# Sixteen of 22 chunks of three feed-forward down-projections as two-by-two blocks with seven block products

## The chip, the cores and the metric

The kernel runs on one core of a Trainium2 chip. Its time is the device time of one execution in microseconds (us). Engines are called by their full names here; in rows, PE is TensorE's products and PEld its weight loads, DVE is VectorE, ACT ScalarE, POOL GpSimd and SP SyncE, which issues most of the DMAs.

## What is computed

Four layers over 256 tokens of width 1024. Each layer has a token mixer (forgetting attention, a state-space layer, mean pooling, forgetting attention again) and then a SwiGLU feed-forward of width 2816; behind each comes a LayerNorm of the scaled residual:

```python
def swiglu(x, w1, w3, w2):
    return (jax.nn.silu(x @ w1) * (x @ w3)) @ w2
    ...
        h = layer_norm(DN_ALPHA * h + m, ln_g[i, 0], ln_b[i, 0])
        h = layer_norm(DN_ALPHA * h + swiglu(h, ffn_w1[i], ffn_w3[i], ffn_w2[i]), ln_g[i, 1], ln_b[i, 1])
```

All is float32.

## The kernel before

Weights come as 370 tiles of 128x1024, 512 KB each, in the order of their use. SyncE loads them into four places `raw`. A float32 value is multiplied as two halves of type float32r: ScalarE rounds a tile to its high half (`hi`, L615), VectorE subtracts that from the tile for the low half (`lo`, L998), and TensorE makes three products, high by high, high by low and low by high. Activations are split in the same way. The halves of a tile lie in `whi` and `wlo` (four places) or in `ext` (four more); which, and whose use frees it, is worked out once by `ring()`. SyncE reloads a `raw` place when the low half of its tile is made; so in layers 1 to 3 the split runs `AHEAD` = 4 tiles further ahead of TensorE than in layer 0.

Each engine's program is written out by hand, and engines wait for each other on counting semaphores: `w_hi` and `w_lo` count tiles rounded and subtracted, `w_used` those TensorE is done with. `hi_to`, `lo_to` and `split_to` split tiles in order up to a number.

**Feed-forward** (`ffn` on each engine). The 2816 hidden channels are 22 chunks of 128. A chunk has two up tiles, `up1` into bank 4 and `up3` into bank 5 (`fm`, L1603 to L1605: 24 products of 256 columns each), and one down tile (`tm`, L1612 to L1618: 12 of 512 columns, for two token blocks and two halves of the width, added up in banks 0 to 3 over all chunks). Chunks 0 and 1 are made token by token (`four_tiles`, L1721) as the LayerNorm delivers, and their `h` is turned (`h_turned`, L1775). Then come `up1(2)`, `up3(2)`, `down(0)`, `down(1)`, and from chunk 3 on up, up and the chunk before's down. ScalarE makes `silu` of bank 4 (L695), VectorE multiplies it by bank 5 into `hval` (`gate`, L1146), ScalarE rounds that to `hhi`, VectorE subtracts for `hlo` (L1150). `up1(c)` waits for chunk c-1's silu, since it writes the same bank, and `up3(c)` for chunk c-1's gate. The last three down tiles stand bank by bank in `tm_end` (L1655), so that VectorE can add bank after bank to the scaled residual in `x_tm` (`residual`, L1014) and begin the LayerNorm.

**GpSimd** works out the state-space tables (`s5_parameters`, `s5_turns`) in layer 0 and issues a few DMAs; in layers 1 to 3 it computes nothing but one copy. In layer 0, VectorE also makes these tables: nine scalings (`s5_scale`) from the attention on, and 48 pieces (`s5_tables`), three a chunk, in the feed-forward. In the attention (`fox`) ScalarE and VectorE copy the values from banks 0 to 3 to `vt` in step 0 of the pairs of heads, behind other copies.

## Time and profile before

| | us |
|---|---|
| runs, median (lowest to highest of 3) | 1180.45 (1180.45 to 1181.71) |
| the profiled execution's own time | 1180.47 |
| its span, first to last instruction | 1178.7 |
| TensorE busy in it | 1157.2 |
| VectorE busy | 819.7 |
| ScalarE busy | 599.1 |
| GpSimd busy | 158.2 |

The span is divided into 40 slices of 29.5 us in the page's second part. Products on TensorE overlap, so the time from one product's start to the next one's start says what it costs, not its own duration. The mean granted clock of TensorE is 0.998 of full speed.

### The profile page before, as it was taken

The numbers are of one execution on the slowest core, as the hardware profiler recorded it, in microseconds if no ns is written. First come the engines' busy times: TensorE is split into PE (matmuls) and PEld (weight loads), VectorE is DVE, ScalarE is ACT, GpSimd is POOL, SyncE is SP. The second block draws the span as 40 slices with busy tenths as digits, with TensorE's granted clock in tenths as the row PEclk, the third lists the DMA queues.
The fourth block names the chain that finished last, engine by engine and source line by source line (L and its number), as shares of the span: only waits on it lengthen the run. The fifth ranks groups of instructions, "written<-read, shape, count | busy, mean of one in ns | idle before, by whom it ended". The sixth has DMA issues, their size and how long they took to land.

```text
span 1178.7 us, 20443 instructions
## 1 busy us (share of the span) xinstructions
PE 1157.2 (98%) x8266; PEld 1037.6 (88%) x8266; DVE 819.7 (70%) x1265; ACT 599.1 (51%) x945; POOL 158.2 (13%) x212
## 2 busy tenths in 40 slices
PE   9999999999999999999999999999999999999996
PEld 7898799999977778999998889999979988999996
DVE  7788899989868687455456776454587767654545
ACT  6776454554445456354444555444438664544441
POOL 0640089102690000000000000000010000000000
PEclk9999999999999999999999999999999999999999
DMA  6685554655676558565654657656537334865640
GB/s 241 211 294 184 162 195 150 200 184 169 199 202 215 179 179 291 183 221 179 204 166 161 196 179 234 197 179 199 189 107 236 125 108 158 271 186 190 189 152 36
DMA packets 63974, 221.02 MB, mean 188 GB/s; under 512 B 8068, under 2 KB 9988, under 8 KB 63368
## 3 DMA queue, kind: packets, MB, share of 16 engines
q1 hardware_dynamic: 57224, 202.57, 52.7%
q0 software_dynamic: 5648, 15.73, 4.3%
q10 hardware_dynamic: 1008, 1.41, 0.4%
q8 instruction: 66, 1.08, 0.4%
q14 instruction: 28, 0.23, 0.1%
HBM read 211.03 MB, written 7.60 MB: 185 GB/s over the span
## 4 chain that ended last, share of the span: by engine, by line
PE 88%; DVE 8%; ACT 1%; DMA 1%; issue 1%; SPq 0%; DVEq 0%; ACTq 0%
PE bank L1603 15%; PE bank L1605 14%; PE bank L1604 14%; PE bank L1612 8%; PE bank L1614 8%; PE bank L1618 8%; PE bank L1721 4%; PE bank L1655 4%; DVE wlo L998 2%; DMA raw<-in_w 1%; PE bank L1910 1%; PE bank L1583 1%; PE bank L1756 1%; PE bank L1892 1%; PE bank L1921 1%
## 5 line engine op out<-in xcount | busy, mean ns | idle before, releaser
L998 DVE TENSOR_TENSOR wlo<-raw,whi 128x1024 fp32r<-128x1024 f32 x227 | 287.4, 1272 | 59.0 <-ACT whi L615 57.7
L615 ACT ACTIVATE whi<-raw 128x1024 fp32r<-128x1024 f32 x227 | 238.8, 1056 | 74.2 <-PE bank L1618 39.0
L1603 PE MATMUL bank<-xboth,whi 128*128 128x256 f32 x936 | 263.8, 282 | 0.0
L1604 PE MATMUL bank<-xboth,whi 128*128 128x256 f32 x936 | 261.9, 280 | 0.0
L1605 PE MATMUL bank<-xboth,wlo 128*128 128x256 f32 x936 | 261.9, 280 | 0.0
L998 DVE TENSOR_TENSOR ext<-raw,ext 128x1024 fp32r<-128x1024 f32 x142 | 172.4, 1222 | 42.6 <-ACT ext L615 42.4
L1605 PEld LDWEIGHTS bank<-xboth,wlo 128*128 128x128 f32 x936 | 178.5, 191 | 0.0
L1603 PEld LDWEIGHTS bank<-xboth,whi 128*128 128x128 f32 x936 | 175.8, 188 | 2.6 <-issue 0.9
L1604 PEld LDWEIGHTS bank<-xboth,whi 128*128 128x128 f32 x936 | 175.8, 188 | 1.4
L615 ACT ACTIVATE ext<-raw 128x1024 fp32r<-128x1024 f32 x142 | 148.5, 1055 | 44.4 <-DMA raw<-in_w 22.6
L1603 PE MATMUL bank<-xboth,ext 128*128 128x256 f32 x600 | 169.5, 282 | 1.1 <-DVE ext L998 0.7
L1605 PE MATMUL bank<-xboth,ext 128*128 128x256 f32 x600 | 168.0, 280 | 0.0
L1604 PE MATMUL bank<-xboth,ext 128*128 128x256 f32 x600 | 168.0, 280 | 0.0
L1146 DVE TENSOR_TENSOR hval<-bank,silu 128x256 f32<-128x256 f32 x80 | 33.9, 423 | 171.8 <-PE bank L1605 171.6
L1603 PEld LDWEIGHTS bank<-xboth,ext 128*128 128x128 f32 x600 | 112.7, 188 | 4.1 <-issue 2.0
L1605 PEld LDWEIGHTS bank<-xboth,ext 128*128 128x128 f32 x600 | 114.5, 191 | 0.0
L1604 PEld LDWEIGHTS bank<-xboth,ext 128*128 128x128 f32 x600 | 112.7, 188 | 1.0
L700 ACT ACTIVATE hhi<-hval 128x256 fp32r<-128x256 f32 x72 | 30.1, 418 | 135.0 <-DVE hval L1146 133.0
L695 ACT ACTIVATE silu<-bank 128x256 f32<-128x256 f32 x80 | 30.6, 382 | 103.6 <-PE bank L1605 103.6
L582 POOL DMA_DIRECT2D slot<-in_ln_row x16 | 8.6, 543 | 452.5 <-DVE x_tm L1070 401.1
L1612 PE MATMUL bank<-whi,hhi 128*128 128x512 f32 x188 | 58.1, 390 | 0.1
L1614 PE MATMUL bank<-wlo,hhi 128*128 128x512 f32 x188 | 57.9, 389 | 0.0
(385 smaller groups left out, 1963.7 us busy)
## 6 DMA issues: line engine op xcount, KB each, us to landing
raw<-in_w SPq DMA_DIRECT2D x370, 512.0 KB, 4.2
slot<-in_ln_row POOLq DMA_DIRECT2D x16, 512.0 KB, 5.9
toep<-slot POOLq DMA_DIRECT2D x8, 512.0 KB, 9.3
toepA<-toep SPq DMA_DIRECT2D x2, 1024.0 KB, 5.8
BT<-toep SPq DMA_DIRECT2D x2, 1024.0 KB, 6.8
x_tm<-in_x SPq DMA_DIRECT2D x2, 512.0 KB, 5.1
slot<-in_s_B SPq DMA_DIRECT2D x2, 512.0 KB, 4.5
slot<-in_s_C SPq DMA_DIRECT2D x2, 512.0 KB, 5.0
```

The lines of the kernel that those rows point to most:

```text
L615: nc.scalar.activation(hi_of(c), raw[:, c % RAW, :], ACT.Copy).then_inc(w_hi, 1)
L695: nc.scalar.activation(silu[:, :], bank[4][:, 0:SEQ], ACT.Silu).then_inc(silu_ready, 1)
L998: V.tensor_tensor(lo_of(c), raw[:, c % RAW, :], hi_of(c).bitcast(F32), ALU.subtract).then_inc(w_lo, 1)
L1146: V.tensor_tensor(hval[:, :], bank[5][:, 0:SEQ], silu[:, :], ALU.mult).then_inc(h_ready, 1)
L1603: mm(dst, wh, bhi[:, kc, :], start=(i == 0), stop=False)
L1604: mm(dst, wh, blo[:, kc, :], start=False, stop=False)
L1605: ins = mm(dst, wl, bhi[:, kc, :], start=False, stop=(i == len(chunks) - 1))
L1612: mm(banks[2 * m + j][:, :], a_hi[:, cols], hi_of(c)[:, j * HALF:(j + 1) * HALF], start=first, stop=False)
L1614: mm(banks[2 * m + j][:, :], a_hi[:, cols], lo_of(c)[:, j * HALF:(j + 1) * HALF], start=False, stop=False)
L1618: ins = mm(banks[2 * m + j][:, :], a_lo[:, cols], hi_of(c)[:, j * HALF:(j + 1) * HALF], start=False, stop=last)
L1655: return mm(banks[b][:, :], (a_lo if lo_act else a_hi)[:, cols], (lo_of if lo_w else hi_of)(c)[:, half], start=False, stop=stop)
L1721: return mm(out, x[:, kc, m * P:(m + 1) * P], w[:, 0:4, kc * P:(kc + 1) * P], start=start, stop=stop)
```

## The change

It concerns the down-projections of layers 1, 2 and 3. Chunks 0 to 15 are taken two by two. For a pair, `h` is a block matrix of two token blocks by two chunks, and the weights one of two chunks by two halves of the width. The product of two such matrices is made from seven block products instead of eight, of sums of blocks:

- GpSimd makes four sums of weight blocks, 128x512 each, out of the `raw` places (`weight_sums`); ScalarE and VectorE split them in two steps (`sums_high`, `sums_low`) into `shi` and `slo`, which hold a pair's seven weight blocks, once. The third of the eight blocks of the two down tiles (`b12`) is used in sums only, so of the first tile only half is split (`width`).
- VectorE makes four sums of 128x128 blocks of `h` (`pair_sums`); the eight blocks in `hs` are split in one piece (`pair_high`, `pair_low`) into one of two places.
- TensorE makes `seven(p)` behind the up tiles of chunk 2p + 3: seven times three products of 512 columns. Six of the seven are added up in banks 0, 1, 2, 3, 6 and 7 over the eight pairs; the last goes to bank 5, which `up3` uses too, and VectorE adds it to `x_tm` behind each pair (`second_product`).
- After the last pair VectorE and ScalarE combine the banks (`first_sums`, `other_sums`) and scale the residual there, so that `residual` only adds. Chunks 16 to 21 are as before, and begin in banks 0 to 3 when these are read.
- SyncE reloads the two `raw` places of a pair when GpSimd has made all its sums (`sums_made`).

In layer 0's attention the copies to `vt` move ahead of the other copies, the last tiles of the output projection are split earlier, and the scalings 4 to 8 move: 4 to the end of the attention, 5 and 6 behind the two turned halves, 7 and 8 among the 50 pieces. The rest of layer 0 is as it was.

```diff
+SEVEN = 8
...
+    def up_at(l, c):
+
+        if l > 0 and c < FCH - 3:
+            return 2 * c if c < 2 else 6 * (c // 2) - 2 + 2 * (c % 2)
+        return 2 * c if c < 3 else 3 * c - 1 if c < FCH - 2 else 2 * c + FCH - 4
+
+    def down_at(l, c):
+
+        if l > 0 and c < 2 * SEVEN:
+            return 6 * (c // 2) + 8 + c % 2
+        if l > 0 and c < FCH - 4:
+            return 6 * SEVEN + 6 + c - 2 * SEVEN
+        return 6 + c if c < 2 else 3 * c + 4 if c < FCH - 4 else T_FFN - FCH + c
+
+    seven_of = {starts[l] + MIX_TILES[MIXERS[l]] + down_at(l, c): ((l - 1) * SEVEN + c // 2, c % 2)
+                for l in range(1, layers) for c in range(2 * SEVEN)}
...
+            if c in seven_of:
+                pair, second = seven_of[c]
+                place.append(None)
+                before.append(c - 9 if pair % SEVEN == 0 else c - 5 - second)
+                continue
...
+        def width(c):
+
+            return HALF if c in seven_of and seven_of[c][1] == 0 else D
...
+                if c - RAW in seven_of:
+                    sp.wait_ge(sums_made, 2 * seven_of[c - RAW][0] + 2)
...
+            def weight_sums(l, p):
+
+                a = starts[l] + MIX_TILES[MIXERS[l]] + down_at(l, 2 * p)
+                i = (l - 1) * SEVEN + p
+                for c in (a, a + 1):
+                    pool.wait_ge(raw_landed[c % RAW], 16 * (c // RAW + 1))
+                b11, b12 = (raw[:, a % RAW, j * HALF:(j + 1) * HALF] for j in range(2))
+                b21, b22 = (raw[:, (a + 1) % RAW, j * HALF:(j + 1) * HALF] for j in range(2))
+                if i > 0:
+                    pool.wait_ge(sum_lo, 2 * i)
+                step(TT(sums[:, 0, :], b12, b11, ALU.subtract))
+                TT(sums[:, 1, :], b22, b12, ALU.subtract).then_inc(sums_made, 1)
+                step(TT(sums[:, 2, :], b22, sums[:, 0, :], ALU.subtract))
+                TT(sums[:, 3, :], sums[:, 2, :], b21, ALU.subtract).then_inc(sums_made, 1)
 
...
+                def silu_of(c):
+
+                    act.wait_ge(h_ready, E0 + c)
+                    act.wait_ge(w_used, T0 + up_at(l, c) + 1)
                     nc.scalar.activation(silu[:, :], bank[4][:, 0:SEQ], ACT.Silu).then_inc(silu_ready, 1)
...
+                def pair_high(p):
+
+                    i = (l - 1) * SEVEN + p
+                    act.wait_ge(hs_set, i + 1)
+                    nc.scalar.activation(hs_hi[:, p % 2, :, :].rearrange("p a t -> p (a t)"), hs[:, :, :].rearrange("p a t -> p (a t)"),
+                                         ACT.Copy).then_inc(hs_hi_set, 1)
+
+                def sums_high(p, h):
+
+                    act.wait_ge(sums_made, 2 * ((l - 1) * SEVEN + p) + h + 1)
+                    nc.scalar.activation(shi[:, 3 + 2 * h:5 + 2 * h, :].rearrange("p a d -> p (a d)"),
+                                         sums[:, 2 * h:2 * h + 2, :].rearrange("p a d -> p (a d)"), ACT.Copy).then_inc(sum_hi, 1)
+
+                def with_sevens():
+
+                    silu_half(0)
+                    split_to(T0 + 5)
+                    act.wait_ge(w_used, T0 + 4)
+                    act.wait_ge(h_ready, E0 + 1)
+                    silu_half(1)
+                    split_to(T0 + 7)
+                    pair_high(0)
+                    for p in range(SEVEN):
+                        at = T0 + up_at(l, 2 * p + 2)
+                        split_to(at + 5)
+                        sums_high(p, 0)
+                        silu_of(2 * p + 2)
+                        sums_high(p, 1)
+                        split_to(at + 7)
+                        if p == SEVEN - 1:
+                            h_high(2 * p + 2)
+                        silu_of(2 * p + 3)
+                        split_to(at + 8)
+                        if p == SEVEN - 1:
+                            h_high(2 * p + 3)
+                        else:
+                            pair_high(p + 1)
+                        split_to(at + 9)
+                    act.wait_ge(w_used, T0 + down_at(l, 2 * SEVEN - 1) + 1)
+                    nc.scalar.copy(mix[:, 0, :], bank[1][:, :]).then_inc(m1_out, 1)
+                    for c in range(2 * SEVEN + 2, FCH):
+                        chunk(c)
+                    split_to(top)
...
+                        if j == 0 and l == 0:
+                            values_out()
+                        if j > 0 or l == 0:
                             hi_to(tq + 2 + more)
...
+                    if j == PAIRS + 1:
+                        hi_to(T1 + KC - 1)
...
+                    if j == PAIRS:
+                        hi_to(T1 + KC - 2)
...
+                if n % 2 == 1 and n > 1:
+                    step(V.tensor_tensor(x_tm[:, m, cols], src, x_tm[:, m, cols], ALU.add))
...
+                pieces = [lambda i=i: s5_tables(i) for i in range(48)]
+                pieces[24:24] = [lambda: s5_scale(7), lambda: s5_scale(8)]
...
+                def h_block(m):
+
+                    dve.wait_ge(hT_ps, TM * l + m + 1)
+                    mark(V.tensor_copy(hs[:, m:m + 3:2, :], bank[6 + m][:, 0:SEQ].rearrange("p (c t) -> p c t", c=2)))
+
+                def pair_sums(p):
+
+                    if p == 0:
+                        marked()
+                    else:
+                        dve.wait_ge(h_ready, E0 + 2 * p + 2)
+                    mark(V.tensor_tensor(hs[:, 4, :], hs[:, 1, :], hs[:, 3, :], ALU.add))
+                    mark(V.tensor_tensor(hs[:, 5, :], hs[:, 0, :], hs[:, 1, :], ALU.subtract))
+                    marked()
+                    step(V.tensor_tensor(hs[:, 6, :], hs[:, 4, :], hs[:, 0, :], ALU.subtract))
+                    V.tensor_tensor(hs[:, 7, :], hs[:, 2, :], hs[:, 6, :], ALU.subtract).then_inc(hs_set, 1)
+
+                def pair_low(p):
+
+                    dve.wait_ge(hs_hi_set, (l - 1) * SEVEN + p + 1)
+                    V.tensor_tensor(hs_lo[:, p % 2, :, :].rearrange("p a t -> p (a t)"), hs[:, :, :].rearrange("p a t -> p (a t)"),
+                                    hs_hi[:, p % 2, :, :].rearrange("p a t -> p (a t)").bitcast(F32), ALU.subtract).then_inc(hs_lo_set, 1)
...
+                def second_product(p):
+
+                    dve.wait_ge(w_used, T0 + down_at(l, 2 * p + 1) + 1)
+                    if p == 0:
+                        V.scalar_tensor_tensor(x_at(0, 0), x_at(0, 0), ALPHA, bank[5][:, :], ALU.mult, ALU.add).then_inc(m2_read, 1)
+                    else:
+                        dve.wait_ge(m2_read, (l - 1) * SEVEN + p)
+                        V.tensor_tensor(x_at(0, 0), bank[5][:, :], x_at(0, 0), ALU.add).then_inc(m2_read, 1)
+
+                def first_sums():
+
+                    dve.wait_ge(w_used, T0 + down_at(l, 2 * SEVEN - 1) + 1)
+                    dve.wait_ge(m2_read, l * SEVEN)
+                    mark(V.scalar_tensor_tensor(x_at(0, 1), x_at(0, 1), ALPHA, bank[0][:, :], ALU.mult, ALU.add))
+                    dve.wait_ge(m1_out, l)
+                    mark(V.tensor_tensor(mix[:, 1, :], bank[2][:, :], mix[:, 0, :], ALU.add))
+                    mark(V.tensor_tensor(x_at(0, 0), bank[1][:, :], x_at(0, 0), ALU.add))
+                    marked()
+                    V.tensor_tensor(mix[:, 2, :], bank[3][:, :], mix[:, 1, :], ALU.add).then_inc(m_read, 1)
...
+                def with_sevens():
+
+                    gate_half(0)
+                    split_to(T0 + 5)
+                    gate_half(1)
+                    h_block(0)
+                    split_to(T0 + 6)
+                    h_block(1)
+                    pair_sums(0)
+                    split_to(T0 + 7)
+                    pair_low(0)
+                    for p in range(SEVEN):
+                        at = T0 + up_at(l, 2 * p + 2)
+                        if p > 0:
+                            second_product(p - 1)
+                        split_to(at + 5)
+                        sums_low(p, 0)
+                        sums_low(p, 1)
+                        gate(2 * p + 2)
+                        split_to(at + 7)
+                        if p == SEVEN - 1:
+                            gate_lo(2 * p + 2)
+                        split_to(at + 8)
+                        gate(2 * p + 3)
+                        if p < SEVEN - 1:
+                            pair_sums(p + 1)
+                            pair_low(p + 1)
+                        else:
+                            gate_lo(2 * p + 3)
+                        split_to(at + 9)
+                    second_product(SEVEN - 1)
+                    first_sums()
+                    for c in range(2 * SEVEN + 2, FCH):
+                        chunk(c)
+                        if c == 2 * SEVEN + 2:
+                            other_sums()
+                    split_to(top)
...
+                if l > 0:
+                    with_sevens()
+                    return
                 gate_half(0)
                 split_to(T0 + 5)
                 gate_half(1)
                 h_low(0)
+                scale(5)
                 split_to(T0 + 6)
-                scales((6, 7))
                 h_low(1)
-                scales((8,))
+                scale(6)
...
+                    if j == 0 and l == 0:
+                        values_out()
...
-                    if l == 0 and layers > 1 and c == 0:
-                        s5_scale(3)
+                    if l == 0 and layers > 1 and c < 2:
+                        s5_scale(3 + c)
...
+                def seven(p):
+
+                    t, i = T0 + down_at(l, 2 * p), (l - 1) * SEVEN + p
+                    pe.wait_ge(w_lo, t + 2)
+                    pe.wait_ge(hs_lo_set, i + 1)
+                    pe.wait_ge(sum_lo, 2 * i + 2)
+                    for a, w, b in ((0, 0, 1), (7, 2, 0), (3, 6, 6), (4, 3, 7), (6, 5, 2), (5, 4, 3), (2, 1, 5)):
+                        if b == 5:
+                            pe.wait_ge(h_ready, E0 + 2 * p + 4)
+                        mm(bank[b][:, :], hs_hi[:, p % 2, a, :], shi[:, w, :], start=p == 0 or b == 5, stop=False)
+                        low = mm(bank[b][:, :], hs_hi[:, p % 2, a, :], slo[:, w, :], start=False, stop=False)
+                        last = mm(bank[b][:, :], hs_lo[:, p % 2, a, :], shi[:, w, :], start=False, stop=p == SEVEN - 1 or b == 5)
+                    used(low)
+                    used(last)
...
+                if l == 0:
+                    down(0)
+                    down(1)
                 for c in range(3, FCH):
                     up1(c)
                     up3(c)
-                    if c < FCH - 3:
+                    if l > 0 and c % 2 == 1 and c <= 2 * SEVEN + 1:
+                        seven(c // 2 - 1)
+                    if l > 0 and c == 2 * SEVEN + 2:
+                        pe.wait_ge(m_read, l)
+                        down(c - 2)
+                        down(c - 1)
+                    if l == 0 and c < FCH - 3:
                         down(c - 1)
```

**The order at the start of a block.** VectorE in layer 1, from the last LayerNorm piece to chunk 2's gate; `hs` and `hs_lo` are the blocks of `h` and their low halves, `slo` and `sums` those of the weights. Before:

```order
L1024 TENSOR_TENSOR xboth<-bank,xboth 128x2x128 x4
L998 TENSOR_TENSOR wlo<-raw,whi 128x1024
L1133 TENSOR_TENSOR slot<-bank,silu 128x256
...
L1140 TENSOR_TENSOR hlo<-bank,hhi 128x2x128
L998 TENSOR_TENSOR wlo<-raw,whi 128x1024
L998 TENSOR_TENSOR ext<-raw,ext 128x1024 x4
L1146 TENSOR_TENSOR hval<-bank,silu 128x256
```

and now:

```order
L1296 COPY hs<-bank 128x2x128
L1304 TENSOR_TENSOR hs<-hs 128x128
L1305 TENSOR_TENSOR hs<-hs 128x128
L1307 TENSOR_TENSOR hs<-hs 128x128
L1308 TENSOR_TENSOR hs<-hs 128x128
L1129 TENSOR_TENSOR wlo<-raw,whi 128x1024
L1313 TENSOR_TENSOR hs_lo<-hs,hs_hi 128x1024
L1129 TENSOR_TENSOR slo<-raw,shi 128x512
L1129 TENSOR_TENSOR slo<-raw,shi 128x1024
L1319 TENSOR_TENSOR slo<-sums,shi 128x1024 x2
L1287 TENSOR_TENSOR hs<-bank,silu 128x256
```

Between the second turned half and chunk 2's gate stood five subtractions of tiles; now there are four small sums, six subtractions of whole width and one of half.

ScalarE at the same place, up to chunk 2's silu (L695 before, L754 now). Before:

```order
L688 ACTIVATE hhi<-bank 128x2x128
L615 ACTIVATE whi<-raw 128x1024
L615 ACTIVATE ext<-raw 128x1024 x4
L695 ACTIVATE silu<-bank 128x256
L615 ACTIVATE whi<-raw 128x1024
```

and now:

```order
L742 ACTIVATE silu<-bank 128x256
L675 ACTIVATE whi<-raw 128x1024 x2
L778 ACTIVATE hs_hi<-hs 128x1024
L675 ACTIVATE shi<-raw 128x512
L675 ACTIVATE shi<-raw 128x1024
L784 ACTIVATE shi<-sums 128x1024
L754 ACTIVATE silu<-bank 128x256
L784 ACTIVATE shi<-sums 128x1024
```

The silu of chunk 2 now stands behind the rounding of `hs`, of the pair's two tiles and of the first two sums of weights. On TensorE, the two down tiles that stood between `up3(2)` and `up1(3)` are gone from there, and the first `seven` follows `up3(3)`.

## Rows read from the trace of the kernel before

**Rows 1.** The page: busy time of the engines, and the 40 slices of POOL.
```profile
PE 1157.2 (98%) x8266; PEld 1037.6 (88%) x8266; DVE 819.7 (70%) x1265; ACT 599.1 (51%) x945; POOL 158.2 (13%) x212
...
POOL 0640089102690000000000000000010000000000
```

**Rows 2.** By stretch: length; PE, PEld, DVE, ACT, POOL busy (x); PEclk, DMA share, GB/s.
```profile
460.00:612.00 152.00, 152.00 (x1106) 144.03 (x1105) 82.25 (x97) 71.75 (x97) 0.00 (x0) 1.00 0.62 199
```

**Rows 3.** Waits of PE, 450 to 620 us: in total, times, longest.
```profile
PE bank L1603 <- ACT silu L695: 0.2, 1, 0.2
```

**Rows 4.** Timeline of PE, layer 1's start: start, duration.
```profile
449.52 0.38 PE L1775 MATMUL bank<-cst,slot 128*128 128x128 f32 x2
...
452.56 0.62 PE L1612 MATMUL bank<-whi,hhi 128*128 128x512 f32 x2
...
457.55 0.61 PE L1618 MATMUL bank<-whi,hlo 128*128 128x512 f32 x2
```

**Rows 5.** Timeline of DVE, the same stretch.
```profile
452.44 2.35 DVE L998 TENSOR_TENSOR ext<-raw,ext 128x1024 fp32r<-128x1024 f32 x2
...
459.16 0.42 DVE L1146 TENSOR_TENSOR hval<-bank,silu 128x256 f32<-128x256 f32 x1
```

**Rows 6.** Timeline of ACT, the same stretch.
```profile
449.93 0.38 ACT L688 ACTIVATE hhi<-bank 128x256 fp32r<-128x256 f32 x1 [1.57 <-PE bank L1775]
...
451.16 2.00 ACT L615 ACTIVATE ext<-raw 128x1024 fp32r<-128x1024 f32 x2
...
457.89 0.36 ACT L695 ACTIVATE silu<-bank 128x256 f32<-128x256 f32 x1
```

**Rows 7.** By stretch and by line of DVE, 286 to 309 us, POOL at work.
```profile
286.00:309.00 23.00, 23.00 (x292) 22.16 (x291) 22.71 (x17) 11.18 (x16) 21.58 (x12) 1.00 0.56 183
...
L998 DVE TENSOR_TENSOR wlo<-raw,whi 128x1024 fp32r<-128x1024 f32 x8 | 15.6, 1956 | 0.0
L1150 DVE TENSOR_TENSOR hlo<-hval,hhi 128x256 fp32r<-128x256 f32 x3 | 3.2, 1070 | 0.0
L1401 DVE TENSOR_TENSOR CT<-CT,slot 128x1024 f32<-128x1024 f32 x1 | 2.1, 2082 | 0.0
L1150 DVE TENSOR_TENSOR h3lo<-hval,h3hi 128x256 fp32r<-128x256 f32 x1 | 1.5, 1501 | 0.0
L1146 DVE TENSOR_TENSOR hval<-bank,silu 128x256 f32<-128x256 f32 x3 | 1.3, 420 | 0.3 <-PE bank L1605 0.3
```

**Rows 8.** Timeline of POOL in that stretch.
```profile
303.76 1.13 POOL L487 TENSOR_TENSOR slot<-cosT,prm 128x512 f32<-128x512 f32 x1
```

**Rows 9.** By line of DVE: 460 to 600 us; then two of the whole span.
```profile
L998 DVE TENSOR_TENSOR wlo<-raw,whi 128x1024 fp32r<-128x1024 f32 x28 | 34.2, 1223 | 14.8 <-ACT whi L615 14.7
...
L1150 DVE TENSOR_TENSOR hlo<-hval,hhi 128x256 fp32r<-128x256 f32 x18 | 7.5, 418 | 0.0
...
L1014 DVE SCALAR_TENSOR_TENSOR x_tm<-x_tm,bank 128x512 f32<-128x512 f32 x26 | 17.7, 681 | 11.6 <-PE bank L1655 11.6
...
L1193 DVE TENSOR_TENSOR wf_lo<-wf,wf_hi 128x128 fp32r<-128x128 f32 x2 | 0.6, 283 | 0.0
```

**Rows 10.** DMA issues of the page: KB each, median us to landing.
```profile
raw<-in_w SPq DMA_DIRECT2D x370, 512.0 KB, 4.2
```

**Rows 11.** By stretch in layer 0, columns as in rows 2.
```profile
36.00:46.00 10.00, 9.29 (x80) 8.90 (x79) 5.91 (x7) 7.52 (x13) 7.76 (x14) 1.00 0.68 223
...
130.00:160.00 30.00, 28.83 (x180) 25.01 (x179) 27.98 (x40) 15.66 (x25) 10.88 (x13) 1.00 0.48 150
```

**Rows 12.** The chain in layer 0; timelines of DVE and PE at its LayerNorm.
```profile
41.82 1.29 DVE vt L1257 x2
43.11 1.26 DVE ext L998
...
124.65 0.67 DVE L1014 SCALAR_TENSOR_TENSOR x_tm<-x_tm,bank 128x512 f32<-128x512 f32 x1
...
128.00 0.66 PE L1583 MATMUL bank<-cst,x_tm 128*128 128x128 f32 x4 [1.39 <-DVE x_tm L1070]
```

141 lines of the change are left out of this document (95 added, 46 removed).

## The prediction

> **What bounds the kernel now.** I read the page first: TensorE is busy for 1157.2 of 1178.7 us, VectorE for 819.7, ScalarE for 599.1 and GpSimd for 158.2, and GpSimd's slices after the 13th are empty but for one copy [rows 1]. So a feed-forward block of layers 1 to 3 is bound by TensorE, and GpSimd is idle in all three. The stages show it again: from 460 to 612 us TensorE has no gap, while VectorE works 82.25 us and ScalarE 71.75 [rows 2]. Then the list of waits: in the whole of layer 1's block TensorE waits 0.2 us for others [rows 3]. A product taken out there is therefore time won, until another engine takes TensorE's place; what is to be asked is where the others stand when it goes. The timeline of the first microseconds of that block is read for this [rows 5, 6], and GpSimd's last stretch of arithmetic in layer 0 for what it does to VectorE [rows 7, 8].
>
> **What goes.** A chunk of a down-projection is 12 products of 512 columns; two chunks are 24. They start at 452.56, and the 23rd at 457.55: 0.227 us each [rows 4]. A pair now has 21, so 3 x 0.227 = 0.68 us less; 8 pairs in 3 layers: 24 x 0.68 = **-16.3 us**. Each product loads its own weights before and after, so I leave 0.227.
>
> **What comes, for a pair.** GpSimd: four additions of 128x512. VectorE: the two down tiles cost 1024 + 1024 columns of subtraction before and 512 + 1024 + 2 x 1024 now; the hidden pair two of 256 before, four of 128x128 and one of 1024 now; one 512-column sum out of a bank besides. ScalarE likewise rounds 512 + 1024 + 2 x 1024 and 1024. Two 1024-column subtractions back to back take 2.35 us, so one after another 1.14; a sum of bank and `x_tm` takes 0.68 (0.6 in a row of them); 128x128 takes 0.28 [rows 5, 9]. VectorE's own chain for a pair: eight of 1024 (four up tiles, second down tile, two of sums, `hs_lo`) 9.1; half tile 0.6; two gates 0.7; bank sum 0.6; four small ones, of which each of the last two waits for one before it, 1.15; the wait for ScalarE to round `hs` 1.06 and two hand-overs 0.15. Together **13.35 us**. TensorE needs for a pair four up tiles of 2.83 (449.52 to 452.56 is one tile with two transposes ahead [rows 4]) and 21 x 0.227: 16.07 us, 16.75 before. Alone, VectorE would keep up.
>
> **GpSimd beside VectorE.** From 286 to 309 us GpSimd works through twelve 128x512 operations, and VectorE has hardly a gap (22.71 of 23 us) [rows 7]. A 1024-column subtraction takes 1956 ns there instead of 1223, a 256-column one 1070 instead of 418 [rows 7, 9]; one that reads a bank beside one SBUF tile stays at 420. Added up: 8 x 0.73 + 3 x 0.65 + 0.86 + 1.08 = 9.8 us for 12 operations, **0.81 us of VectorE for each** [rows 7]. GpSimd itself takes 1.13 us for one left alone [rows 8] and 1.80 on average in that stretch (21.58 / 12). Nearly all that VectorE does in a pair reads two SBUF tiles, so I take 4 x 0.81 = 3.25 us for a pair: 13.35 + 3.25 = 16.6 us against 16.07. The bounds: nothing, if the additions fall into VectorE's gaps, and 4 x 1.13 = 4.5. Beside this stands a rule: the Trainium skill (SBUF — State Buffer, on the shared port pair) says that a VectorE operation with two SBUF inputs and a GpSimd one that reads SBUF take the shared pair as an exclusive lock for the whole instruction. The trace agrees in which forms suffer, not in the size; by the rule the sum would have the full block, which is a rival below.
>
> **The start of each block, the term that decides.** Before, both down tiles 0 and 1 (5.4 us of products) stood between the up tiles of chunk 2 and of chunk 3; now nothing does. TensorE would like to start chunk 3 at 452.56 and its second up tile at 455.4 (2.83 later). It needs chunk 2's silu for the first and its gate for the second. Before, ScalarE gave that silu at 457.89 and VectorE that gate at 459.16 [rows 5, 6], which was just in time. Now, in the new order and in layer 1's times:
> - the second turned block is there at 449.93, where ScalarE read it before [rows 6]; VectorE copies it by 450.3, and the four small sums end at 451.65;
> - ScalarE rounds `hs` (1.06) until 452.8, then the half tile 0.55, the tile 1.0, the first sums 1.0, and the silu 0.36: **455.7**, so TensorE's first up tile is 3.1 us late;
> - VectorE subtracts tile 7 until 452.8, `hs_lo` 454.0, half tile 454.6, tile 455.7, sums 456.9 and 458.0, gate **458.4**: 3.0 us after 455.4. But GpSimd's four additions begin when tile 9 lands: 4.2 us after tile 5's subtraction, about 451 [rows 10], and VectorE is then busy without a gap, so 3.25 us come on top: gate at 461.7.
> The start costs 6.3 us by the gate; bounds 3.1 (no contention) and 7.6 (full). Layers 2 and 3 have the same order, so 3 x 6.3 = **+18.9 us**. In the seven pairs behind it VectorE's 16.6 against 16.07 gives 7 x 0.5 = 3.7; I take 3.0 since the bank sum (0.6) is not slowed: 3 x 3.0 = **+9.0 us**, bounds 0 and 3 x 7 x 1.8 = 38.
>
> **What else moves.** The sums out of the banks behind the last pair (one ScalarE copy, five VectorE operations, 3.3 us) lie beside chunk 18's two up tiles (5.65 us): nothing, and 0.7 a layer if VectorE comes 3 us late. The six later ones lie beside up tiles, where VectorE has the room that its 82 us in 152 leave [rows 2]. SyncE issues the same 370 loads, up tiles now two chunks ahead of a pair. SyncE must wait for GpSimd's sums before it reloads the two `raw` places: that is a rival. LayerNorm's sums become additions of the same size [rows 9]. In layer 0: the first gate no longer waits behind two scalings; TensorE idled 1.17 us there [rows 11]. The two `vt` copies (1.29 us) leave the chain ahead of the tile subtracted from 43.11 on, where it idled 0.71 [rows 11, 12]. The last output-projection tiles are split earlier, so that LayerNorm's second sum needn't wait until 124.65 behind a late tile; TensorE then idled 1.39 us for it [rows 12], of which I count 1.15. Together **-3.0 us**, bounds -3.3 and 0.
>
> **Sum.** -16.3 + 18.9 + 9.0 - 3.0 = +8.6 us on 1180.47, the profiled execution's own time, which is the median of the runs too (1180.45): **1189 us**. About 0.2% (2.4 us) can be told from no change.
>
> **Rivals.**
> - *The other side, faster:* the price of GpSimd's additions decides. If they slip into VectorE's waits, each start costs 3.1 us and the pairs none: -16.3 + 9.3 - 3.0 = -10.0, **1170.5 us**. For it: GpSimd is busy for 5 to 8 of 16 us here, for 21.58 of 23 in [rows 7], and VectorE has waits of some 2 us in a pair. Against it: at the start VectorE has none. Half the price gives -16.3 + 3 x 4.7 - 3.0 = -5.2. The point from which it turns: 19.3 us to lose in three blocks, 6.4 each, of which 3.1 is certain; above 3.3 us of contention in a block it is slower. I give all this 0.32.
> - *The loop of the weight places, slower still:* SyncE reloads the `raw` places of a pair only when GpSimd has made all its sums. From there to the next sums the chain is: landing 4.2 [rows 10], rounding 1.06, subtraction 1.14, gate 0.34, small sums 1.15, rounding 1.06 and `hs_lo` 1.14 with hand-overs 0.3, up tile 1.14, bank sum 0.6, the next half and full tile 1.74, last addition 1.13, and 2.4 for three additions met on the way: 17.4, less what runs side by side, near 17.0. Then a pair loses 0.9: 7 x 0.9 = 6.3 a block in place of 3.0: +8.6 + 9.9 = 18.5, **1199 us**. I give 0.15.
> - *A full block:* each of GpSimd's additions holds VectorE for its whole 1.13 us [rows 8], 4.5 in place of 3.25: 1.27 more at each of 3 starts and in 21 pairs, +8.6 + 30.5 = 39, **1219 us**. Against it stand the 0.81 of [rows 7]; I give 0.05. This is the rule of the page named above (SBUF — State Buffer, of the Trainium skill) taken at its word.
> - *No change to be told,* the terms cancel within 2.4 us: 0.08.
> - *My forecast,* 1183 to 1195: 0.40.
>
> The range: 8 in 10 reaches from the no-contention end, 1170, to just beyond the loop, 1202; the full block is left out. Faster 0.32, same 0.08, slower 0.60.
>
> **What would show it.** Right: 72 products fewer than 8266 [rows 1], with gaps at three places only, ahead of chunk 3's two up tiles, 6 us together in each block, ended by ScalarE's silu and then VectorE's gate; GpSimd's additions at 1.8 us, VectorE's subtractions beside them near 2.0; a pair every 16.5 us; layer 0's 1.17 us between 130 and 160 [rows 11] gone. Wrong: additions at 1.13 us with VectorE at 1.22, or a gate before 459 in layer 1's times, makes it faster; SyncE waiting on GpSimd with ScalarE idle for landings, and pairs of 17 us, is the loop.

## The result, and the profile after

The changed kernel takes **1218.66 us** in the median (1216.96 to 1224.66, 4 runs); the kernel before, on the same chip, 1180.45 (1180.37 to 1181.71). The ratio is 1.033, 95% interval 1.031 to 1.0349: 38 us slower. The forecast was 1189 (1170 to 1202): the side was right, the size was not.

The page of the changed kernel, busy times as in [rows 1], its chain of waits by engine, and GpSimd's new lines:

```profile
PE 1159.2 (95%) x8194; PEld 1037.7 (85%) x8194; DVE 1013.4 (83%) x1445; ACT 639.6 (53%) x972; POOL 341.1 (28%) x308
...
PE 62%; DVE 13%; POOL 11%; DMA 7%; issue 3%; ACT 3%; POOLq 0%; SPq 0%; DVEq 0%; ACTq 0%
...
L608 POOL TENSOR_TENSOR sums<-raw 128x512 f32<-128x512 f32 x24 | 37.2, 1552 | 233.9 <-DMA raw<-in_w 217.2
```

TensorE has its 72 products fewer (8194 for 8266 in [rows 1]). VectorE is busy 194 us longer, GpSimd 183. TensorE's waits for others, the counterpart of [rows 3] but over the whole span (in total, times, longest):

```profile
PE bank L1856 <- DVE hs L1287: 22.2, 19, 2.2
PE bank L1856 <- ACT silu L754: 12.2, 3, 4.7
PE bank L1856 <- DVE wlo L1129: 2.1, 1, 2.1
```

Three waits for a silu are the three starts. Of the nineteen for the gate (L1287), seventeen lie in the pairs, about 1 us each time, but 2.1 to 2.2 three times and 0.3 once, which [rows 2] and [rows 3] had nothing of; two stand at starts, 0.7 and 1.8 us. The third line is a single wait, in layer 0, that the kernel before did not have.

**The pairs.** The gates of chunks 2, 4, 6 and so on (the even gates) in layer 1 stand at 463.84, 481.12, 498.41, 515.70, 532.97, 550.26 and 568.67 us: a pair every **17.28 us**, once 18.41, where TensorE's own work is 16.07. The chain of waits says what is in the 17.28. One turn of it, in order of time (start, duration, what), without seven pieces of 0.02 to 0.09 us:

```profile
532.97 0.42 DVE hs L1287
533.39 2.28 DVE ext L1129 x2
535.69 4.65 DMA raw<-in_w
540.46 1.36 POOL sums L608
541.89 2.17 POOL sums L609
544.06 1.72 POOL sums L610
545.84 2.16 POOL sums L611
548.02 1.07 ACT shi L784
549.12 0.06 DVE slo L1319
549.18 1.08 issue
550.26 0.42 DVE hs L1287
```

TensorE is not in it. The gate of chunk 2p+2 stands behind the low parts of the sums on VectorE; the two up tiles behind the gate set `raw` places free; those are loaded with the next pair's down tiles (4.65 us); GpSimd then makes their sums (7.54 us from 540.46 to 548.00), ScalarE and VectorE split them, and only then comes the next gate.

**The start of a block.** VectorE in layer 1, the counterpart of [rows 5] (the first turned block is at 448.26 here, 446.56 before), then two stretches:

```profile
453.04 1.37 DVE L1308 TENSOR_TENSOR hs<-hs 128x128 f32<-128x128 f32 x1
454.33 1.21 DVE L1129 TENSOR_TENSOR wlo<-raw,whi 128x1024 fp32r<-128x1024 f32 x1
455.53 2.22 DVE L1313 TENSOR_TENSOR hs_lo<-hs,hs_hi 128x1024 fp32r<-128x1024 f32 x1
457.68 3.97 DVE L1129 TENSOR_TENSOR slo<-raw,shi 128x512 fp32r<-128x512 f32 x2
```

```profile
456.00:460.00 4.00, 1.68 (x8) 1.71 (x9) 4.00 (x3) 2.18 (x4) 3.92 (x3) 0.59 0.38 133
460.00:464.00 4.00, 3.72 (x18) 3.49 (x17) 4.00 (x4) 2.95 (x3) 0.57 (x1) 0.56 0.52 165
```

The stretches have the columns of [rows 2]. From 453.04 on VectorE has no gap, and `hs_lo` and the two `slo` take nearly twice their time without additions beside them (2.22 and 3.97 us for 1.23 and 1.94 in first_sums_narrow below). Between the second turned half and the gate VectorE has five subtractions of whole width and one of half, not six and one as written under the change. The gate of chunk 2 comes at 463.84, 15.58 us after the first turned block. TensorE stands still for most of 456 to 460, and its granted clock is 0.59 and 0.56 there. What the start costs is read from TensorE itself, at the first of the seven products:

```profile
467.22 0.39 PE L2061 MATMUL bank<-shi,hs_hi 128*128 128x512 f32 x1
```

That is 18.96 us behind the first turned block, 18.70 and 18.87 in layers 2 and 3. Without a wait it would be 11.66: `up1(3)` at 6.0 (452.56 against 446.56) and two up tiles of 2.83. So the three starts cost 7.3, 7.0 and 7.2 us.

**Layer 0** came out ahead at first: the 1.17 and 1.39 us of [rows 11, 12] are gone and the block's first transposes start at 139.72 instead of 143.16. Then, with no counterpart before:

```profile
299.03 0.38 PE L1856 MATMUL bank<-xboth,whi 128*128 128x256 f32 x1 [2.14 <-DVE wlo L1129]
```

Behind it the clock is 0.61 from 300 to 304, and 0.58 from 368 to 372. Layer 1's block begins 1.7 us later than before. So 5.1 us are lost behind 139.72, the larger part with the clock: gate_first_low_late (below) has the same layer 0 and the same wait of 2.14 us, but 1.00 from 300 to 304. From the first transposes of layer 0's block to those of layer 1's it is 308.5 us here, 305.3 there and 303.4 before.

### The profile page after: what moved, and what is told of

Its sections match the earlier page's. It is cut to its first block, busy times and chain, and to the rows that moved or that the text cites. A ratio compares the mean times of both kernels' runs of the same rounds, so it can differ in the third digit from the quotient of the medians.

```text
span 1216.8 us, 20715 instructions
## 1 busy us (share of the span) xinstructions
PE 1159.2 (95%) x8194; PEld 1037.7 (85%) x8194; DVE 1013.4 (83%) x1445; ACT 639.6 (53%) x972; POOL 341.1 (28%) x308
## 4 chain that ended last, share of the span: by engine, by line
PE 62%; DVE 13%; POOL 11%; DMA 7%; issue 3%; ACT 3%; POOLq 0%; SPq 0%; DVEq 0%; ACTq 0%
PE bank L1856 8%; PE bank L1857 8%; PE bank L1858 8%; DMA raw<-in_w 7%; PE bank L1865 5%; PE bank L1867 5%; PE bank L1871 5%; PE bank L1974 5%; PE bank L1908 4%; DVE wlo L1129 3%; POOL sums L609 3%; POOL sums L611 3%; POOL sums L610 3%; POOL sums L608 2%; DVE ext L1129 2%
## 5 line engine op out<-in xcount | busy, mean ns | idle before, releaser
L1129 DVE TENSOR_TENSOR wlo<-raw,whi 128x1024 fp32r<-128x1024 f32 x201 | 264.6, 1333 | 28.9 <-ACT whi L675 27.7
L675 ACT ACTIVATE whi<-raw 128x1024 fp32r<-128x1024 f32 x201 | 209.4, 1055 | 46.9 <-PE bank L1871 22.1
L1856 PE MATMUL bank<-xboth,ext 128*128 128x256 f32 x608 | 174.2, 286 | 17.9 <-DVE hs L1287 13.1
L1858 PE MATMUL bank<-xboth,ext 128*128 128x256 f32 x608 | 172.1, 283 | 0.0
L1857 PE MATMUL bank<-xboth,ext 128*128 128x256 f32 x608 | 172.1, 283 | 0.0
L1129 DVE TENSOR_TENSOR ext<-raw,ext 128x1024 fp32r<-128x1024 f32 x120 | 153.1, 1301 | 15.4 <-ACT ext L675 15.2
L675 ACT ACTIVATE ext<-raw 128x1024 fp32r<-128x1024 f32 x120 | 123.8, 1053 | 18.9 <-DMA raw<-in_w 18.5
L608 POOL TENSOR_TENSOR sums<-raw 128x512 f32<-128x512 f32 x24 | 37.2, 1552 | 233.9 <-DMA raw<-in_w 217.2
L784 ACT ACTIVATE shi<-sums 128x1024 fp32r<-128x1024 f32 x48 | 50.8, 1059 | 78.6 <-POOL sums L611 57.5
L1319 DVE TENSOR_TENSOR slo<-sums,shi 128x1024 fp32r<-128x1024 f32 x48 | 77.3, 1621 | 7.6 <-ACT shi L784 6.8
L1129 DVE TENSOR_TENSOR slo<-raw,shi 128x512 fp32r<-128x512 f32 (+1 forms) x48 | 81.6, 1738 | 0.0
L778 ACT ACTIVATE hs_hi<-hs 128x1024 fp32r<-128x1024 f32 x24 | 25.5, 1061 | 86.6 <-DVE hs L1308 86.6
```

Source lines behind the costliest of these rows:

```text
L608: step(TT(sums[:, 0, :], b12, b11, ALU.subtract))
L675: nc.scalar.activation(hi_of(c), raw[:, c % RAW, 0:width(c)], ACT.Copy).then_inc(w_hi, 1)
L784: nc.scalar.activation(shi[:, 3 + 2 * h:5 + 2 * h, :].rearrange("p a d -> p (a d)"), sums[:, 2 * h:2 * h + 2, :].rearrange("p a d -> p (a ...
L1129: V.tensor_tensor(lo_of(c), raw[:, c % RAW, 0:width(c)], hi_of(c).bitcast(F32), ALU.subtract).then_inc(w_lo, 1)
L1319: V.tensor_tensor(slo[:, 3 + 2 * h:5 + 2 * h, :].rearrange("p a d -> p (a d)"), sums[:, 2 * h:2 * h + 2, :].rearrange("p a d -> p (a d)"), ...
L1856: mm(dst, wh, bhi[:, kc, :], start=(i == 0), stop=False)
```

## Experiments: the pairs

Two things can explain 17.28 us, as it seemed at this point. The chain above (theory 1, the reload), or VectorE's own row (theory 2): in 481 to 533 us it works 48.04 of 51.85 us and waits 1.1 a pair for ScalarE's `hs_hi`, which makes it full. Two moves tell them apart; neither changes an instruction.

```diff
 VectorE, loop over p (ScalarE likewise):     gate_first
-    sums_low(p, 0)
-    sums_low(p, 1)
     gate(2 * p + 2)
     split_to(at + 7)
+    sums_low(p, 0)
+    sums_low(p, 1)
```
```diff
 VectorE (ScalarE's pair_high likewise):      low_late
     pair_sums(p + 1)
-    pair_low(p + 1)
     split_to(at + 9)
+    pair_low(p + 1)
```

**gate_first**, the first move alone: the gate and the two up tiles behind it no longer stand behind the sums' low parts. 

> The changed kernel with one thing moved: in each pair of chunks VectorE makes the even gate and the two up tiles behind it before the low parts of the sums, and ScalarE's silu and splits go the same way. GpSimd's work, its stretching of VectorE and all instruction counts stay. Theory 1 (the reload): the pair's 17.28 us is the chain raw tiles landed, GpSimd's four sums 7.75, ScalarE 1.06, low part, gate 0.42, two up tiles 2.28, transfer 4.3 to 4.6, which the reordering cuts; the pair comes down to TensorE's 16.2 or to VectorE's own 17.1, so between 0.2 and 1.1 us a pair in 21 pairs: 1195 to 1214 us. Theory 2 (VectorE is full: 16.0 busy and 1.1 us of waiting for ScalarE's hs_hi in each pair of 17.28): nothing of it changes, the pair stays at 17.1 to 17.3 and the time at 1214 to 1219 us.

Measured: **1197.29 us** (ratio to before 1.0125, 1.0106 to 1.0144), 21 us less than the changed kernel. The six gate distances of layer 1 are 16.03 to 17.80, 16.66 on average. Theory 2 alone had nothing change, so the chain counted; what holds the pairs above 16.07 here this run doesn't say.

**low_late_alone**, the second move alone. 

> The changed kernel with only the second of the two moves: pair_high and pair_low one weight tile later, sums_low still ahead of the even gate. VectorE no longer stands 1.1 us a pair for hs_hi, but the chain raw tiles, GpSimd's sums, sums_low, gate, two up tiles, reload is untouched. If that chain sets the pair of 17.28 us: no change, pair 17.2 to 17.3, 1215 to 1219 us. If VectorE's full row set it: pair 16.2, 1197 us or less.

Measured: **1203.21 us** (1.0170, 1.0147 to 1.0193), against my expectation from theory 1 of no change. The chain is still there, but in layer 1 a turn of it takes 16.44 us (16.78 once; in layers 2 and 3 five of the twelve take 17.65 to 17.97). Of the 0.84 us less, 0.80 is in GpSimd's additions:

```profile
537.64 1.41 POOL L608 TENSOR_TENSOR sums<-raw 128x512 f32<-128x512 f32 x1 [9.71 <-DMA raw<-in_w]
539.13 1.30 POOL L609 TENSOR_TENSOR sums<-raw 128x512 f32<-128x512 f32 x1
540.38 1.75 POOL L610 TENSOR_TENSOR sums<-raw,sums 128x512 f32<-128x512 f32 x1
542.22 2.15 POOL L611 TENSOR_TENSOR sums<-sums,raw 128x512 f32<-128x512 f32 x1
```

L609 takes 1.30 in place of 2.17. VectorE's rows beside it, first here, then in the changed kernel:

```profile
538.63 0.69 DVE L1333 TENSOR_TENSOR x_tm<-bank,x_tm 128x512 f32<-128x512 f32 x1 [0.72 <-PE bank L2064]
```
```profile
540.58 2.31 DVE L1129 TENSOR_TENSOR wlo<-raw,whi 128x1024 fp32r<-128x1024 f32 x1
```

Here VectorE, ahead by the wait it no longer has, is at the sum out of a bank when L609 begins; there it is in the middle of a subtraction of two SBUF tiles. So the two theories were one too few: the reload chain sets the pair, and its length depends on what VectorE happens to do beside the four additions.

**gate_first_low_late**, both. 

> The same, and the low part of the eight h blocks is made one weight tile later on VectorE (its high part one tile later on ScalarE), so that VectorE does not stand 1.1 us in each pair for ScalarE's hs_hi. If both the reload chain and VectorE's full row were near 17.2, this and not the run before brings the pair to TensorE's 16.2: 21 pairs x 1.0 = 21 us less than the changed kernel, 1195 to 1200 us. Theory 1 alone expects this run equal to the one before within 2 us. If GpSimd kept VectorE out for the whole of each addition, the pair would stay above 17 us here too, 1214 us or more.

Measured: **1185.64 us** (1.0038, 1.0024 to 1.0051), 11.7 us below gate_first where theory 1 alone had no difference, and below the 1195 to 1200 expected of both. In layer 1 the gates are 16.03, 16.11, 16.06, 16.07, 16.07 and 16.06 us apart: TensorE's own pace, for which the prediction had worked out 16.07. Three pairs by stretch, columns as in [rows 2], here and in the changed kernel:

```profile
474.28:522.52 48.24, 48.24 (x353) 45.74 (x353) 44.46 (x49) 27.78 (x34) 22.55 (x12) 1.00 0.57 196
```
```profile
481.12:532.97 51.85, 48.90 (x351) 45.85 (x351) 48.04 (x49) 27.58 (x34) 22.39 (x12) 1.00 0.51 182
```

GpSimd does as much as before; VectorE does the same 49 instructions in 3.6 us less, since other ones meet the additions. Where the gain lies is read from TensorE's own products, from one group of seven to the next. The medians are 33.0 us apart, the profiled spans 34.6. Of these, the seven distances in three blocks give 29.2 (122.80, 122.77 and 122.67 us against 112.73, 113.78 and 112.55), the starts 1.7 (first of the seven products at 18.45, 18.25 and 18.16 for 18.96, 18.70 and 18.87), and 3.4 stand ahead of layer 1. The first gate is earlier by 6.8 us in all (13.36, 13.16 and 13.06 us after the first turned block for 15.58, 15.33 and 15.50), but that is mostly its new place in VectorE's order: TensorE then waits for the sums' low parts, 1.47 us in layer 2.

**narrow_sums.** GpSimd's additions take 32 columns of 512 behind one memset, in the changed kernel's own order; the other columns are left out of the result. 

> The changed kernel, but GpSimd's four additions of a pair take 32 columns, not 512 (the sums of the other columns are left at zero, so part of the products is left out of the result; every other instruction is the same size). It takes away both what GpSimd does to VectorE (3.2 us a pair) and most of GpSimd's own 7.75 us of the reload chain. All theories that blame GpSimd's additions expect TensorE's pace in the pairs, 16.1 to 16.3 us: 21 x 1.0 = 21 us less than the changed kernel, and at the three starts another 1 to 3 us each, so 1190 to 1196 us. If the block's loss had nothing to do with GpSimd, 1216 us or more. What is left at each start then is ScalarE's and VectorE's own chain and the low clock; I expect a gap of 2 to 3 us ahead of chunk 3 against 3.8 to 4.7.

Measured: **1181.63 us** (0.9996, 0.9984 to 1.0008), more than expected was won. The distances are 16.07 from the second on; three pairs of VectorE's work nearly without contention:

```profile
477.33:525.53 48.20, 48.20 (x353) 45.75 (x353) 37.72 (x48) 27.29 (x34) 2.98 (x12) 1.00 0.61 194
```

Against its 37.72 us, the twelve full additions cost VectorE 10.3 us in the changed kernel, **0.86 each**, and 6.7 in gate_first_low_late, 0.56 each (one instruction less falls into this stretch, so up to 0.1 of each is that). The gap ahead of chunk 3 in layer 1 was 3.45 us, more than the 2 to 3 expected.

**added_sums.** The kernel before, with 32 idle additions in layer 1's block:

```diff
+for p in range(8):
+    pool.wait_ge(w_lo, T0 + down_at(2 * p + 2) + 1)
+    step(TT(q[0], q[2], q[3], ALU.subtract))
...
```

> The kernel before with 32 idle GpSimd additions of 128x512 (four for each two chunks, 8 times) in the feed-forward block of layer 1 alone, on a buffer that nothing else uses there; nobody waits for them. If GpSimd's additions only slow VectorE's instructions and VectorE has room (busy 13 to 14 us of 17 there): the time stays at 1181 to 1183 us, VectorE's low parts beside them take 1.7 to 2.4 us in place of 1.22, and the price is about 0.8 us of VectorE for each addition, 26 us in the block. If the additions alone cost TensorE time by delaying low parts, the block loses several us: 1184 us or more.

Measured: **1181.47 us** (0.9998, 0.9982 to 1.0013): no cost. By stretch, here and in the kernel before:

```profile
450.00:610.00 160.00, 160.00 (x1154) 151.32 (x1153) 104.84 (x102) 77.34 (x103) 56.47 (x32) 1.00 0.62 205
```
```profile
450.00:610.00 160.00, 159.76 (x1156) 150.90 (x1155) 87.25 (x102) 76.70 (x103) 0.00 (x0) 1.00 0.65 207
```

VectorE pays 17.6 us for 32 additions, 0.55 each, not the 26 expected, and TensorE nothing. Here, where neither VectorE nor GpSimd stands in the chain, the contention costs no time.

## Experiments: the start

**first_sums_narrow.** gate_first_low_late with 32-column additions in the first pair of each block only, the other columns left out. 

> gate_first_low_late, but the first pair of each of the three blocks has GpSimd's additions on 32 columns, behind a memset of the whole sums (those products are left out of the result; the seven later pairs are as they were). If GpSimd's additions beside VectorE are what stretches the start (hs_lo 2.3 us in place of 1.2, slo x2 4.0 in place of 1.9, the tile ahead of them 2.3 in place of 1.2: 4.3 us): the first seven products start 2 to 4 us earlier in each block, 1174 to 1180 us. If VectorE's own row and ScalarE's set it: 1184 to 1186 us.

Measured: **1175.29 us** (0.9951, 0.9939 to 0.9963), 10.3 us below gate_first_low_late: **3.4 us a block** are GpSimd's additions beside VectorE. The first gate is 9.21 us behind the first turned block for 13.36, in the same order, and the seven products start 4.2, 3.9 and 3.1 us earlier in the three blocks. VectorE, then GpSimd:

```profile
453.81 1.22 DVE L1132 TENSOR_TENSOR wlo<-raw,whi 128x1024 fp32r<-128x1024 f32 x1
455.02 1.23 DVE L1316 TENSOR_TENSOR hs_lo<-hs,hs_hi 128x1024 fp32r<-128x1024 f32 x1
456.17 1.94 DVE L1132 TENSOR_TENSOR slo<-raw,shi 128x512 fp32r<-128x512 f32 x2
```
```profile
452.96 1.81 POOL L609 MEMSET sums<- 128x2048 f32 x1 [9.27 <-DMA raw<-in_w]
454.86 0.28 POOL L611 TENSOR_TENSOR sums<-raw 128x32 f32<-128x32 f32 x1
455.22 1.15 POOL L612 TENSOR_TENSOR sums<-raw 128x32 f32<-128x32 f32 x1
```

In gate_first_low_late the same three of VectorE take 2.32, 2.29 and 3.99 us: 4.2 us for four additions, 1.05 each, nearly the 1.13 that an addition alone takes [rows 8].

**fill_products.** gate_first_low_late with needless products in the start's two gaps:

```diff
+    if l > 0 and c == 3:
+        fill(16)
     up1(c)
+    if l > 0 and c == 3:
+        fill(20)
     up3(c)
```

> gate_first_low_late with 16 and 20 needless products of 256 columns (1.8 and 2.3 us at the full clock) on a free bank in the two gaps ahead of chunk 3's up tiles, to see what the low clock behind the gaps costs. If the fall of the granted clock to 0.5 to 0.7 near 456 to 464 us is part of a start's price, the clock stays at 1.00 there and 1 to 1.5 us a block come back: 1181 to 1183 us. If VectorE's low parts set the start anyway (they end at 463.2 us in layer 1), nothing comes back: 1185 to 1187 us.

Measured: **1186.06 us** (1.0047, 1.0028 to 1.0066), the same. The clock is indeed back (PEclk is the third number from the right; first here, then without the products):

```profile
456.00:460.00 4.00, 4.00 (x36) 4.00 (x36) 4.00 (x4) 3.07 (x4) 1.59 (x1) 1.00 0.36 120
```
```profile
456.00:460.00 4.00, 1.19 (x5) 1.22 (x6) 4.00 (x5) 2.74 (x4) 1.25 (x1) 0.85 0.36 130
460.00:464.00 4.00, 4.00 (x23) 3.78 (x23) 4.00 (x4) 2.12 (x2) 0.00 (x0) 0.72 0.88 311
```

But VectorE ends the low parts of the first sums at the same time, and TensorE waits for those instead: 1.07 us ahead of the first seven products. A low clock ahead of a wait cost nothing here. Behind the last wait it does cost, as own_first_early shows below.

**start_early, all_mended, all_mended_2, all_mended_3.** Four tries to reorder the start, on gate_first_low_late; the last three with the 48-place list of layer 0 (below). start_early and all_mended put ScalarE's silu of chunk 2 ahead of the split of the eighth tile, the two others behind it; all four make VectorE's gate of chunk 2 right behind `pair_low(0)`; all_mended_3 also makes the first sums' low parts ahead of the two up tiles.

> gate_first_low_late with the start of each block reordered: ScalarE makes the silu of chunk 2 ahead of the h blocks' high part, VectorE the gate of chunk 2 ahead of the splits of the pair's down tiles. Theory (the gaps ahead of chunk 3's tiles are ScalarE's and VectorE's order, and GpSimd's stretch beside it): the gaps of 1.8 to 3.9 and 1.7 to 2.9 us go; TensorE comes earlier to the first seven products and waits there for the low parts of the sums instead, which VectorE still reaches at the same time, about 18.3 us after the first h_turned. So 0.5 to 2 us a block, 1180 to 1184 us against 1185.6. Rival (VectorE's row alone sets the start): the wait only moves ahead of L2062, no gain within 1 us.

> start_early and the 48-place list of layer 0 together, with all of the original change's seven-product blocks. If the terms add: gate_first_low_late 1185.6, less 2 to 4 for layer 0, less 1 to 4 for the starts: 1178 to 1182 us, no slower than the kernel before (1180.9).

> all_mended with the silu of chunk 2 moved behind the split of the block's eighth tile, ahead of the h blocks' high part only. In all_mended it stood ahead of two splits and waited 2.7 us for TensorE, which pushed VectorE's four small h sums beside GpSimd's additions. I expect no gap ahead of up1(3), one of about 1 us ahead of up3(3), and a wait of 3 to 5 us ahead of the first seven products, ended by the low parts of the sums: 1178 to 1183 us, against 1189.4.

> all_mended_2 with the sums of the first pair made ahead of the two up tiles behind them, so that the first seven products start about 2.3 us earlier; the tiles of the second pair are then reloaded 2.3 us later. If the start is set by VectorE's row up to the sums' low parts: 1 to 2 us a block less than all_mended_2, 1175 to 1180 us. If the second pair's sums then come late: the same time as all_mended_2 within 2 us, with the wait ahead of the second seven products.

Measured: **1192.82** (1.0088, 1.0056 to 1.0119), **1189.36** (1.0066, 1.0043 to 1.0088), **1185.27** (1.0032, 1.0015 to 1.0050) and **1185.12 us** (1.0027, 1.0010 to 1.0045). Only the second case of the last expectation held. In start_early the silu waits 2.73 us for TensorE with two splits behind it, and VectorE's small `h` sums fall beside the additions:

```profile
453.97 1.26 DVE L1309 TENSOR_TENSOR hs<-hs 128x128 f32<-128x128 f32 x1
455.27 1.25 DVE L1310 TENSOR_TENSOR hs<-hs 128x128 f32<-128x128 f32 x1
```

They take 1.26 and 1.25 for 0.29. In all_mended_2 the gate of layer 1 is early (8.39 us behind the first turned block; 11.58 and 11.63 in layers 2 and 3) and the first up tiles follow at once, but TensorE then waits 6.10 us for L1328, the sums' low parts: the seven products start 18.04 us behind the first turned block, 18.45 in gate_first_low_late. In these orders VectorE's row sets the start. The chunk-4 gate is even later, 30.44 us for 29.39; the granted clock is 0.50 from 460 to 464 there. In all_mended_3 that gate comes at 27.30, and the next distances are 17.62, 17.00 and 17.03: the later reload of the second pair takes it back.

**own_first_sums, own_first_early.** VectorE makes the first pair's sums itself, GpSimd starts with the second pair:

```diff
 GpSimd
-    for p in range(SEVEN):
+    for p in range(1, SEVEN):
         weight_sums(l, p)
 VectorE
     split_to(T0 + 7)
+    first_weight_sums()
     pair_low(0)
```

> mended, but VectorE makes the first pair's four sums of each block itself, between the split of the eighth tile and the h blocks' low part; GpSimd makes those of the seven later pairs. VectorE's row at the start gains four additions of 128x512 (about 0.6 us each, 2.5) and loses GpSimd's stretch of it (4.1 us measured: 13.36 us from the first h_turned to the first gate against 9.21 in first_sums_narrow). If that is all: 1.6 us a block less than mended (1183.9): 1178 to 1181 us. If the later low part of the h blocks then holds TensorE up at the gate of chunk 2: 1182 to 1186 us.

> The same with the silu of chunk 2 ahead of the h blocks' high part and the gate of chunk 2 ahead of the down tiles' splits (as in all_mended_2). With GpSimd silent at the start I expect no gap ahead of up1(3) and a short one ahead of up3(3), and the first seven products at the same time as in own_first_sums, since VectorE's row ends at the same place: within 1.5 us of it, 1177 to 1181 us.

Measured: own_first_sums **1178.42 us** (0.9981, 0.9969 to 0.9993), own_first_early **1182.59** (1.0017, 1.0007 to 1.0026). An addition takes VectorE 0.6 us in a row of them, and nothing beside it is stretched:

```profile
451.22 0.68 DVE L1330 TENSOR_TENSOR sums<-raw 128x512 f32<-128x512 f32 x1
...
453.26 0.69 DVE L1333 TENSOR_TENSOR sums<-sums,raw 128x512 f32<-128x512 f32 x1
453.87 1.22 DVE L1320 TENSOR_TENSOR hs_lo<-hs,hs_hi 128x1024 fp32r<-128x1024 f32 x1
```

The first gate is at 11.66 us for 13.36, the chunk-4 gate at 27.59. own_first_sums is the only version with the seven products that computes everything and is below the kernel before, by 0.2%, which is at the edge of what can be told. It also contains layer 0's part in its 48-place form, which alone gives 0.9972 (layer0_48, below): the seven products themselves have won nothing that can be told even here. In a block they save 5.4 us of products, and the start, with the first seven at 16.75 us for 11.66 without a wait, takes 5.1 back.

own_first_early is 4 us slower though its seven products start at the same place as expected, 16.88, 16.78 and 16.79 us behind the first turned block for 16.75 three times. TensorE waits longer ahead of them, and its granted clock then falls to half while it works on them, with nobody to wait for (the wait, then the stretch behind it here and in own_first_sums, where the wait is 1.48 us):

```profile
461.00 0.47 PE L2087 MATMUL bank<-shi,hs_hi 128*128 128x512 f32 x1 [3.21 <-DVE slo L1340]
```
```profile
461.00:465.00 4.00, 4.00 (x11) 3.14 (x12) 3.90 (x8) 2.12 (x2) 0.72 (x1) 0.57 0.82 286
```
```profile
461.85:465.85 4.00, 4.00 (x18) 3.29 (x19) 3.90 (x8) 1.94 (x2) 1.08 (x1) 1.00 0.84 295
```

From the first seven products to the next it is 17.78, 17.80 and 17.77 us in the three blocks, for 16.19, 16.16 and 16.17: 1.6 us a block, 4.8 in all. So here the low clock is the price. That is read from the traces; no run took the clock alone away here.

## Experiments: layer 0

**layer0_alone.** Only the layer-0 part, on the kernel before:

```diff
+pieces = [lambda i=i: s5_tables(i) for i in range(48)]
+pieces[24:24] = [lambda: s5_scale(7), lambda: s5_scale(8)]
```

> The kernel before with only the layer-0 part of the change (values copied out earlier, first splits of the feed-forward block earlier, scalings moved, two of them among the table pieces, which become 50). Theory A (the two added pieces push three table pieces beside GpSimd's twelve additions): a gap of about 2 us near 295 to 300 us on TensorE, ended by VectorE's low part, a low clock behind it, and a total of 1180 to 1183 us, no gain. Theory B (the gap came from the seven-product blocks or the tile order): no such gap, 1177 us.

Measured: **1181.29 us** (1.0001, 0.9989 to 1.0012), and the gap is there without any seven-product block:

```profile
298.72 0.38 PE L1624 MATMUL bank<-xboth,whi 128*128 128x256 f32 x1 [2.14 <-DVE wlo L1011]
```

**layer0_48.** The two scalings are made together with pieces 22 and 23:

```diff
+pieces[22] = lambda: scaled_table(22, 7)
+pieces[23] = lambda: scaled_table(23, 8)
```

> The layer-0 part alone on the kernel before, as in layer0_alone, but the two scalings are made together with pieces 22 and 23, so that the list keeps its 48 places and every later table piece stands where it stood before. If the added places are the cause, the gap of 2.14 us at 298.7 us is gone, the 3 us gained ahead of it stay, and the time is 1176 to 1179 us, 2 to 4 us under layer0_alone. If the gap comes from the splits moved to the block's start, it stays and the time is that of layer0_alone, 1181 us.

Measured: **1178.78 us** (0.9972, 0.9960 to 0.9984). Stretches of both, columns as before, first this one:

```profile
288.00:304.00 16.00, 16.00 (x236) 15.35 (x235) 15.71 (x13) 8.37 (x13) 15.37 (x9) 1.00 0.58 197
```
```profile
288.00:304.00 16.00, 13.86 (x108) 13.19 (x108) 16.00 (x11) 6.13 (x9) 15.29 (x10) 1.00 0.41 134
```

TensorE's gap is gone. Theory A stands: two places more in the list push table pieces of VectorE beside GpSimd's twelve operations of [rows 7]. There are three of them in layer0_alone, and one in layer0_48 and in the kernel before:

```profile
284.89 2.08 DVE L1418 TENSOR_TENSOR CT<-lam,slot 128x1024 f32<-128x1024 f32 x1
...
289.13 2.08 DVE L1420 TENSOR_TENSOR slot<-lam,slot 128x1024 f32<-128x1024 f32 x1
...
293.14 2.33 DVE L1422 TENSOR_TENSOR CT<-CT,slot 128x1024 f32<-128x1024 f32 x1
```

Against the kernel before, this is the lowest ratio of all that computes everything, and it has no seven products in it; own_first_sums (0.9981) can't be told from it.

**mended.** gate_first_low_late with that list. 

> gate_first_low_late with the 48-place list of layer 0 and nothing else. If the two gains add, 1185.6 less the 3.4 us by which layer0_48 and layer0_alone differ: 1181 to 1183.5 us, the same as the kernel before within 2 us. If the low clock in layer 0 and in the S5 block hides it: 1185 to 1187 us.

Measured: **1183.92 us** (1.0030, 1.0013 to 1.0047). The interval overlaps that of gate_first_low_late, so whether layer 0's gain adds in full is not told. In its profiled execution layer 1 begins 2.0 us earlier (442.85 for 444.89), and 1.4 of them are lost behind a wait of 2.30 us ahead of the first seven products, with the clock at 0.58 from 460 to 464 (17.69 us to the next seven for 16.28, while they start at 18.02 for 18.45).

## Why the prediction missed

Measured against the terms of the sum, in the order of the prediction; starts and pairs by TensorE's own products:

- **What goes, -16.3:** right in number (72 products), and 16.07 us for TensorE's work in a pair is the distance at which the mended kernels run.
- **The start, +18.9:** the reasoning held; measured are 7.3, 7.0 and 7.2 us, 21.6 in all. The end of the gate of chunk 2 was forecast 15.1 us behind the first turned block (461.7 against 446.56) and came at 16.0, 15.7 and 15.9. The 3.25 us a block put down for contention are 3.4 in first_sums_narrow. In the changed kernel the low parts of the sums stand ahead of that gate; a wait of TensorE for them shows only where the gate was moved ahead, as in fill_products and all_mended_2.
- **The pairs, +9.0: this is the term that failed.** The prediction weighed VectorE's 16.6 against TensorE's 16.07 as two totals, for seven pairs a block. Measured are 10.3, 10.3 and 10.2 us over seven distances of 16.07, **30.8 in all**. What set the pair was a chain from one even gate to the next: the low parts of two up tiles set two `raw` places free, the next down tiles are loaded there (4.65), GpSimd makes all four sums one after another (7.54), and their low parts stand ahead of the next even gate. Taking the gate out from behind them (gate_first) and moving `pair_low` besides brought the pair to 16.07 with the same instructions.
- **The rival that came near,** the loop of the weight places with 0.15, names the same buffers and a price of 17.0, near 17.28, but another chain. It goes through SyncE's wait for GpSimd's sums, the small sums and `hs_lo`, none of which is in the chain read from the trace, and has one addition in series and 2.4 us for contention met on the way, where four stand in series and contention stretches them by 3.0 (7.54 against 4 x 1.13). The sign it named, SyncE waiting for GpSimd, is there (26.0 us in five pairs) and proves nothing: in gate_first_low_late, at TensorE's pace, it is 35.0. That its price came near is luck.
- **0.81 us for an addition:** the right size for the changed kernel (0.86), and not a constant: 0.55 in added_sums, 0.56 in gate_first_low_late, 1.05 at a start.
- **Layer 0, -3.0:** won as worked out (3.4 us by 139.72), then lost, to a wait that the diff doesn't show and the list's length makes, and with the low clock behind it: of 5.1 us lost behind 139.72, 3.2 are missing in gate_first_low_late, which has the wait but not the low clock. The prediction had read [rows 7], the very stretch, for another purpose, and never asked what the change pushes into it.
- **The sum of the miss, 29.6:** 21.8 in the pairs (30.8 for 9.0), 4.7 in layer 0 (-3.0 forecast, +1.7 read), 2.7 at the starts (21.6 for 18.9), and 0.4 that these terms leave.

The rival of the full block gave 1219 us, and 1218.66 was measured. That is luck: its price of 1.13 for each addition is not met in the pairs (0.86), and gate_first_low_late runs all the same additions at TensorE's pace.

The exclusion that it starts from, though, is shown. At the start VectorE and GpSimd take turns: a 32-column addition takes 0.28 us alone and 1.15 beside a subtraction of 1.23, which is not slowed itself; small VectorE sums of 0.29 take 1.25 beside a 512-column addition; beside a memset by GpSimd (1.81 us) a subtraction keeps its 1.22. The Trainium skill (SBUF — State Buffer, Who interferes with whom) says just this, an exclusive lock held for the whole instruction, between a VectorE operation with two SBUF inputs and a GpSimd one that reads SBUF. The trace agrees, 1.05 of 1.13 us, where VectorE has no gap. Where it has gaps the time lost is less (0.55 in added_sums); that a turn then often falls into a wait which is there anyway is my reading, and no run tested it.

## What to carry to other kernels

When a change adds work to two idle engines, compare more than their totals with the bound engine's: write down each chain that goes from a buffer's release back to the same buffer's release, and what stands ahead of each link in its engine's order. Here two moves of lines, with not one instruction changed, were worth 33 of the 38 us. Read what such a move gives from the bound engine's own instructions: a moved gate is earlier by its new place alone. And where work is moved into a list that others share, look at what the longer list pushes, and beside whom it comes to stand.

## What the runs showed of the hardware

- A GpSimd addition that reads SBUF and a VectorE operation on two SBUF tiles exclude each other for a whole instruction, whatever their sizes: 128x128 on VectorE 0.29 to 1.25 us, 128x32 on GpSimd 0.28 to 1.15. A sum out of a bank and one SBUF tile keeps its 0.69 us beside an addition (low_late_alone), and a subtraction its 1.22 beside a GpSimd memset of 1.81.
- The granted clock fell to half behind some of TensorE's gaps and not behind others of the same length. Behind the same gap of 2.14 us in layer 0 it is 0.57 to 0.64 from 300 to 304 in the traces of the changed kernel, gate_first, narrow_sums and start_early, and 1.00 in those of low_late_alone, gate_first_low_late, first_sums_narrow, fill_products and layer0_alone; what decides it stays open.
- What the low clock costs depends on what comes next. Ahead of another engine's row it cost nothing (fill_products held it at 1.00 and won nothing); behind the last wait, on the seven products, it cost 1.6 us a block (own_first_early).
